# Splitting 544 tokens as 320 + 224 in place of 272 + 272 in a one-core decoder layer step

## The reference

```
h1 = LN1(ALPHA*x  + 0.5*SwiGLU_1(x))      # 1024 -> 2816 (twice) -> 1024
h2 = LN2(ALPHA*h1 + Mixer(h1))
y  = LN3(ALPHA*h2 + 0.5*SwiGLU_2(h2))
Mixer: z = h1 @ w_in -> pooled channels u, q (8 heads x 64), k, v (2 x 64), two gate vectors
  A: trailing means over 2/4/8/16 tokens minus the token, a 128x128 map per group, projection
  B: attention over the token and its 128 predecessors, rotary positions, sinks, projection
  out = (sigmoid(gA)*A + sigmoid(gB)*B) @ w_out
```

## Time and profile before

| | |
|---|---|
| runs timed | 1168.05 us and 4292.71 us |
| profiled execution: span | 1165.2 us |
| PE busy | 1136.7 us, 98% |
| PE weight loads busy | 1110.7 us, 95% |
| DVE busy | 556.8 us, 48% |
| ACT busy | 376.4 us, 32% |
| POOL busy | 149.6 us, 13% |
| mean granted TensorE clock | 0.991 |
| HBM traffic | 87 GB/s mean |

### The profile page before, as it was taken

How to read it: one execution, slowest core, us unless ns; L and a number is a source line. 1 busy time by engine, 2 the same in 40 slices (tenths; PEclk the granted TensorE clock), 3 DMA queues, 4 the chain that set the end, 5 groups by cost and what they waited for, 6 DMA issues and landing times.

```text
span 1165.2 us, 21801 instructions
## 1 busy us (share of the span) xinstructions
PE 1136.7 (98%) x8774; PEld 1110.7 (95%) x8774; DVE 556.8 (48%) x957; ACT 376.4 (32%) x676; POOL 149.6 (13%) x171
## 2 busy tenths in 40 slices
PE   6999999999999999999999999799999999999996
PEld 6999999999999989998899999699999999999994
DVE  3343433243443486877455555943443324444347
ACT  5222222122133334374442243422222222223334
POOL 2000000000002468400000015500000000000240
PEclk9999999999999989999999999999999999999998
DMA  9233441233333243221132332133243213234102
GB/s 250 73 91 90 124 134 56 73 91 91 95 107 88 70 120 74 76 64 37 46 91 73 96 105 78 50 91 89 78 119 94 73 56 109 79 90 132 43 1 77
DMA packets 191416, 101.16 MB, mean 87 GB/s; under 512 B 15129, under 2 KB 189453, under 8 KB 191320
## 3 DMA queue, kind: packets, MB, share of 16 engines
q1 hardware_dynamic: 189136, 95.77, 28.8%
q0 software_dynamic: 2208, 4.38, 1.2%
HBM read 97.63 MB, written 3.68 MB: 87 GB/s over the span
## 4 chain that ended last, share of the span: by engine, by line
PE 91%; DVE 6%; ACT 2%; issue 1%; DMA 0%; SPq 0%; DVEq 0%; ACTq 0%
PE psum L1157 29%; PE psum L1159 29%; PE psum L1158 28%; DVE y L868 1%; DVE act_lo L875 1%; PE psum L1341 1%; DVE y L849 1%; DVE ring_lo L788 1%; DVE stat L854 1%; PE psum L1357 1%; ACT ring_hi L528 0%; DMA xin<-in_x_prompt 0%; PE psum L1373 0%; DVE y L813 0%; PE psum L1269 0%
## 5 line engine op out<-in xcount | busy, mean ns | idle before, releaser
L1157 PE MATMUL psum<-act_hi,ring_hi 128*128 128x272 f32 x1824 | 532.0, 292 | 8.8 <-DVE act_lo L875 4.9
L1159 PE MATMUL psum<-act_hi,ring_lo 128*128 128x272 f32 x1824 | 530.3, 291 | 0.0
L1158 PE MATMUL psum<-act_lo,ring_hi 128*128 128x272 f32 x1824 | 527.0, 289 | 0.0
L1157 PEld LDWEIGHTS psum<-act_hi,ring_hi 128*128 128x128 f32 x1824 | 345.6, 189 | 17.7 <-DVE act_lo L875 9.3
L788 DVE TENSOR_TENSOR ring_lo<-raw,ring_hi 128x1024 fp32r<-128x1024 f32 (+1 forms) x170 | 202.0, 1189 | 305.7 <-ACT ring_hi L528 258.8
L1158 PEld LDWEIGHTS psum<-act_lo,ring_hi 128*128 128x128 f32 x1824 | 346.3, 190 | 0.0
L1159 PEld LDWEIGHTS psum<-act_hi,ring_lo 128*128 128x128 f32 x1824 | 345.4, 189 | 0.0
L528 ACT ACTIVATE ring_hi<-raw 128x1024 fp32r<-128x1024 f32 (+1 forms) x170 | 172.4, 1016 | 234.7 <-PE psum L1159 232.6
L568 ACT ACTIVATE tmp_a<-psum 128x272 f32<-128x272 f32 x184 | 73.2, 398 | 424.4 <-PE psum L1159 363.6
L1157 PE MATMUL psum<-hid_hi,ring_hi 128*128 128x272 f32 x512 | 148.6, 290 | 0.0
L1158 PE MATMUL psum<-hid_lo,ring_hi 128*128 128x272 f32 x512 | 147.0, 287 | 0.0
(11 more groups left out here) (185 smaller groups left out, 1184.6 us busy)
## 6 DMA issues: line engine op xcount, KB each, us to landing
raw<-in_ffn_w SPq DMA_DIRECT2D x176, 256.0 KB, 3.2
raw<-in_ffn_w SPq DMA_DIRECT2D x32, 512.0 KB, 4.0
raw<-in_w_in SPq DMA_DIRECT2D x52, 256.0 KB, 3.3
ext_raw<-in_ffn_w SPq DMA_DIRECT2D x32, 192.0 KB, 4.1
raw<-in_w_out SPq DMA_DIRECT2D x16, 256.0 KB, 3.2
raw<-in_w_pool_out SPq DMA_DIRECT2D x16, 128.0 KB, 2.3
raw<-in_w_attn_out SPq DMA_DIRECT2D x16, 128.0 KB, 2.7
xin<-in_x_prompt SPq DMA_DIRECT2D x3, 512.0 KB, 5.7
```

Source lines behind the costliest of these rows:

```text
L1157: pe.matmul(o, weights(s, k, True), x_hi[:, k, tok(c)], start=k == 0, stop=False)
L1158: pe.matmul(o, weights(s, k, True), x_lo[:, k, tok(c)], start=False, stop=False)
L1159: ins = pe.matmul(o, weights(s, k, False), x_hi[:, k, tok(c)], start=False, stop=k == kn - 1)
```

## The change

The cut between the chunks moves from token 272 to token 320. Chunk 0 has 320 tokens, chunk 1 has 224: 192 of the prompt and the 32 decoding ones. The token tiles of the transposes become 128, 128, 64 and 128, 64, 32 in place of 128, 128, 16 and 128, 112, 32. Scratch tiles get the width of the longer chunk and each use takes only its part. One ScalarE instruction that copied both chunks of a pooled group at once becomes two, one for each chunk. The number of matmuls, their order and their operand types stay.

```diff
-C = T // 2
+CUT = 320
+CHUNK = (CUT, T - CUT)
+CM = max(CHUNK)
...
-TOK_TILES = [(0, 128, 0), (128, 128, 0), (256, 16, 0), (272, 128, 1), (400, 112, 1), (512, 32, 1)]
+TOK_TILES = [(0, 128, 0), (128, 128, 0), (256, 64, 0), (320, 128, 1), (448, 64, 1), (512, 32, 1)]
...
-            return slice(c * C, c * C + C)
+            return slice(c * CUT, c * CUT + CHUNK[c])
...
-                    o = psum[:, bank, 0:C]
+                    o = psum[:, bank, 0:CHUNK[c]]
                     pe.matmul(o, weights(s, k, True), x_hi[:, k, tok(c)], start=k == 0, stop=False)
...
-                dve.tensor_tensor(tmp_v[:, c, :], psum[:, bank_of(at, c), 0:C], tmp_a[:, c, :], ALU.mult) \
+                dve.tensor_tensor(tmp_v[:, c, 0:CHUNK[c]], psum[:, bank_of(at, c), 0:CHUNK[c]], tmp_a[:, c, 0:CHUNK[c]], ALU.mult) \
...
-                        act.activation(scaled[:, slot, :].rearrange("p (c t) -> p c t", c=2), prod, ACT.Copy,
-                                       scale=pscale[:, g:g + 1]).then_inc(att_free, 1)
-                        act.activation(pz_hi[:, g, :].rearrange("p (c t) -> p c t", c=2), prod, ACT.Copy,
-                                       scale=pscale[:, g:g + 1]).then_inc(att_free, 1)
+                        for dst in (scaled[:, slot, :], pz_hi[:, g, :]):
+                            for c in range(2):
+                                ins = act.activation(dst[:, tok(c)], psum[:, 4 + 2 * i + c, 0:CHUNK[c]], ACT.Copy,
+                                                     scale=pscale[:, g:g + 1])
+                            ins.then_inc(att_free, 1)
...
-                        n = SEQ - C
+                        n = SEQ - CUT
...
-                        pe.matmul(psum[:, 4 + 2 * i, 0:C], w, z[:, BUF:BUF + C], start=True, stop=True)
-                        pe.matmul(psum[:, 5 + 2 * i, 0:n], w, z[:, BUF + C:BUF + SEQ], start=True, stop=True)
-                        ins = pe.matmul(psum[:, 5 + 2 * i, n:C], w, seg, start=True, stop=True)
+                        pe.matmul(psum[:, 4 + 2 * i, 0:CUT], w, z[:, BUF:BUF + CUT], start=True, stop=True)
+                        pe.matmul(psum[:, 5 + 2 * i, 0:n], w, z[:, BUF + CUT:BUF + SEQ], start=True, stop=True)
+                        ins = pe.matmul(psum[:, 5 + 2 * i, n:n + NS], w, seg, start=True, stop=True)
```

More of the change, by code:

```diff
@@ L142, in program @@
         soft = sb("soft", [P, 2, 6, H])
-        fsum = sb("fsum", [P, 2, C])
-        stat = sb("stat", [P, 2, C])
+        fsum = sb("fsum", [P, 2, CM])
+        stat = sb("stat", [P, 2, CM])
         table = sb("table", [P, 3])
[L146 to L149, removed]
+        p0 = sb("p0", [P, 4 * T])
+        tmp_a = sb("tmp_a", [P, 2, CM])
+        tmp_v = sb("tmp_v", [P, 2, CM])
+        sqs = [p0[:, 4 * CUT * c:4 * (CUT + CHUNK[1] * c)].rearrange("p (o t) -> p o t", o=4) for c in range(2)]
         tmp_r, scratch = stat[:, 1, :], stat[:, 0, 0:max(WINDOWS)]
@@ L430, in norm_sums @@
                         pool.wait_ge(shift_mm[c], l + 1)
-                    first = y[:, 0, tok(c)] if o == 1 else fsum[:, c, :]
-                    pool.tensor_tensor(fsum[:, c, :], first, y[:, o, tok(c)], ALU.add).then_inc(fsum_done[c], 1)
+                    total = fsum[:, c, 0:CHUNK[c]]
+                    first = y[:, 0, tok(c)] if o == 1 else total
+                    pool.tensor_tensor(total, first, y[:, o, tok(c)], ALU.add).then_inc(fsum_done[c], 1)
                 for k in range(1 if o == 3 else o, o + 1) if 3 <= o < KD - 1 else ():
@@ L436, in norm_sums @@
                         pool.wait_ge(sqsum_done[c], (KD - 2) * l + k - 1)
-                    total = sq[:, 4 * c, :]
-                    pool.tensor_tensor(total, total, sq[:, sq_slot(c, k), :], ALU.add).then_inc(sqsum_done[c], 1)
+                    total = sqs[c][:, 0, :]
+                    pool.tensor_tensor(total, total, sqs[c][:, sq_slot(c, k), :], ALU.add).then_inc(sqsum_done[c], 1)
             def all_norm_sums(l):
@@ L662, in epilogue @@
                     act.wait_ge(evac[c], u)
-                    act.activation(vT[:, tok(c)], psum[:, bank, 0:C], ACT.Copy).then_inc(evac[c], 1)
+                    act.activation(vT[:, tok(c)], psum[:, bank, 0:CHUNK[c]], ACT.Copy).then_inc(evac[c], 1)
                 elif U_GA <= m < U_PA:
@@ L666, in epilogue @@
                     act.wait_ge(evac[c], u)
-                    act.activation(m1[:, m - U_GA, tok(c)], psum[:, bank, 0:C], ACT.Sigmoid).then_inc(evac[c], 1)
+                    act.activation(m1[:, m - U_GA, tok(c)], psum[:, bank, 0:CHUNK[c]], ACT.Sigmoid).then_inc(evac[c], 1)
                 elif m >= U_GB and not is_proj(m):
@@ L813, in residual @@
                 dve.scalar_tensor_tensor(out=y[:, o, tok(c)], in0=y[:, o, tok(c)], scalar=factor,
-                                         in1=tmp_a[:, c, :], op0=ALU.mult, op1=ALU.add).then_inc(y_done[c], 1)
+                                         in1=tmp_a[:, c, 0:CHUNK[c]], op0=ALU.mult, op1=ALU.add).then_inc(y_done[c], 1)
             def deviation(l, c, o):
@@ L840, in norm_center @@
                 bank = stat_bank(l, c)
-                s = stat[:, c, :]
-                step(dve.tensor_tensor(s, psum[:, bank, 0:C], s, ALU.subtract))
+                s = stat[:, c, 0:CHUNK[c]]
+                step(dve.tensor_tensor(s, psum[:, bank, 0:CHUNK[c]], s, ALU.subtract))
                 step(dve.tensor_tensor(s, s, s, ALU.mult))
-                dve.tensor_tensor(s, psum[:, bank ^ 1, 0:C], s, ALU.subtract).then_inc(var_done[c], 1)
-                mean = psum[:, bank:bank + 1, 0:C].broadcast_to([P, 4, C])
+                dve.tensor_tensor(s, psum[:, bank ^ 1, 0:CHUNK[c]], s, ALU.subtract).then_inc(var_done[c], 1)
+                mean = psum[:, bank:bank + 1, 0:CHUNK[c]].broadcast_to([P, 4, CHUNK[c]])
                 for i in range(2):
@@ L953, in rotate @@
                     to = q + half if q % HD == 0 else q - half
-                    ins = dve.tensor_tensor(tmp_r[to:to + half], x[q:q + half, :],
+                    ins = dve.tensor_tensor(tmp_r[to:to + half, 0:CHUNK[c]], x[q:q + half, :],
                                             cos_sin[q:q + half, 1, tok(c)], ALU.mult)
                 step(ins)
-                dve.tensor_tensor(dst, tmp_v[:, c, :], tmp_r, ALU.add).then_inc(evac[c], 1)
+                dve.tensor_tensor(dst, tmp_v[:, c, 0:CHUNK[c]], tmp_r[:, 0:CHUNK[c]], ALU.add).then_inc(evac[c], 1)
             def epilogue(m, c):
@@ L971, in epilogue @@
                     dve.wait_ge(evac[c], u)
[L972 removed]
+                    prod = psum[:, bank_of(u, c), 0:CHUNK[c]]
+                    v = tmp_v[:, c, 0:CHUNK[c]]
                     if m < U_GB:
@@ L980, in epilogue @@
                         dve.wait_ge(m_done[c], o)
-                    dve.tensor_tensor(tmp_v[:, c, :], prod, tmp_a[:, c, :], ALU.mult).then_inc(evac[c], 1)
+                    dve.tensor_tensor(v, prod, tmp_a[:, c, 0:CHUNK[c]], ALU.mult).then_inc(evac[c], 1)
                     dve.wait_ge(evac[c], u + 1)
-                    step(dve.tensor_tensor(tmp_v[:, c, :], tmp_v[:, c, :], m1[:, o, tok(c)], ALU.add))
-                    step(dve.tensor_copy(m_hi[:, o, tok(c)], tmp_v[:, c, :]))
-                    dve.tensor_tensor(m_lo[:, o, tok(c)], tmp_v[:, c, :], m_hi[:, o, tok(c)], ALU.subtract) \
+                    step(dve.tensor_tensor(v, v, m1[:, o, tok(c)], ALU.add))
+                    step(dve.tensor_copy(m_hi[:, o, tok(c)], v))
+                    dve.tensor_tensor(m_lo[:, o, tok(c)], v, m_hi[:, o, tok(c)], ALU.subtract) \
                         .then_inc(m_done[c], 1)
@@ L1168, in shift @@
                 pe.wait_ge(consts_in, 16 * CONST_DMAS)
-                pe.matmul(psum[:, stat_bank(l, c), 0:C], mean_w[:, 0:P], fsum[:, c, :], start=True, stop=True) \
+                pe.matmul(psum[:, stat_bank(l, c), 0:CHUNK[c]], mean_w[:, 0:P], fsum[:, c, 0:CHUNK[c]], start=True, stop=True) \
                     .then_inc(shift_mm[c], 1)
@@ L1176, in stats @@
                 pe.wait_ge(fsum_done[c], (KD - 2) * (l + 1))
-                pe.matmul(psum[:, bank, 0:C], mean_w[:, 0:P], fsum[:, c, :], start=True, stop=False)
+                pe.matmul(psum[:, bank, 0:CHUNK[c]], mean_w[:, 0:P], fsum[:, c, 0:CHUNK[c]], start=True, stop=False)
                 pe.wait_ge(sqsum_done[c], (KD - 2) * (l + 1))
-                pe.matmul(psum[:, bank ^ 1, 0:C], mean_w[:, 0:P], sq[:, 4 * c, :], start=True, stop=False)
+                pe.matmul(psum[:, bank ^ 1, 0:CHUNK[c]], mean_w[:, 0:P], sqs[c][:, 0, :], start=True, stop=False)
                 pe.wait_ge(y_done[c], y_before(l) + KD)
-                pe.matmul(psum[:, bank, 0:C], mean_w[:, 0:P], y[:, KD - 1, tok(c)], start=False, stop=True)
+                pe.matmul(psum[:, bank, 0:CHUNK[c]], mean_w[:, 0:P], y[:, KD - 1, tok(c)], start=False, stop=True)
                 pe.wait_ge(sq_done[c], sq_op(l, KD - 1))
-                pe.matmul(psum[:, bank ^ 1, 0:C], mean_w[:, 0:P], sq[:, sq_slot(c, KD - 1), :], start=False,
```

(1 more changed line is left out.)

37 lines of the change are left out of this document (18 added, 19 removed).

## The result

The changed kernel takes 1195.59 us, median of two runs (1195.16 to 1196.02). Against the comparable runs of the kernel before it takes 1.0241 times as long, interval 1.022 to 1.0261: it is slower. The median of the two runs shown before, 2730.38 us, is no measure for this, since its run of 4292.71 us is left out of the ratio as not comparable. A second measurement, with seven runs of the kernel before on the same chip (median 1166.89 us), gives 1195.47 us and a ratio of 1.0247, interval 1.0229 to 1.0265. The profiled span grew from 1165.2 to 1194.2 us, by 29.0 us.

The account below looks back on a forecast made before the run. TensorE's matmul stream, with 91% of the chain of waits, was taken as the bound. Pairs 35.5 + norms 1.8 - tail 0.8 + start 0.4 = 37 us on 1168 gave 1205 us; range 1170 to 1232, likeliest 1188 to 1225.

Parts of the forecast that it names:

- wait saved at the second norm: TensorE reaches chunk 1's first tile 1.5 us later; 1.3 us of that taken as saved wait at each norm.
- The pair: Matmuls of 320 and 224 columns: 146.5 + 113 = 259.5 ns against 251.0, 8.5 more, times 4176: +35.5 us.
- The start: At the kernel's start the third token tile has 64 tokens, not 16, so its two copies take longer: +0.4 us.
- The norms: Mixer and second FFN starts: chunk 0's longer tiles and lost cover, less wait saved, 0.9 us each: +1.8 us.
- The tail: Chunk 1's bare norm at the end, 6.9 us, shortens 1.0 us; 0.2 returns through chunk 0's scaling: -0.8 us.
- Rival 1: fp32r load and matmul pair has a 125.5 ns floor: +44 us, 1213; upper bound +88 us, 1257; chance 0.22.
- Rival 2: 12 ns surplus comes from stream and load nearly tying at 272 columns: pair 246 ns, -21 us, 1148 to 1150; chance 0.17.
- Rival 3: Longer tiles draw out the lower clock after the norms: 5 to 15 us above forecast, up to 1220; chance 0.06.
- Rival 4: 224-column fp32r matmuls fall to fp32 speed, 373 ns each: +1.1 ms; chance 0.02.

Follow-up runs that it names:

- second profile: Profile of the changed kernel (320 + 224) measured once more, unchanged: 1195.47 us against 1166.89 us for the kernel before; profiled span 1193.4 us.

## Why the prediction was right or wrong

I predicted 1205 us, +37; it was 1195.6, about +28. The direction and the mechanism were right and the size was 9 us too high. The step that failed is the price of the pair, and in it the 113 ns for 224 columns; a second one is the wait saved at the second norm.

- **The pair.** I took 146.5 for 320 columns and 113 for 224, 8.5 ns more for the pair. Measured 146.6 and 111.5, 7.0 ns: 29 us in place of 35.5. The term that was off is the 3 ns that I added to the load's 110 for reading the moving operand beside it; 1.5 were there. The distances of loads are 111.5 ns beside 224 fp32r columns and 109.4 beside 96, which would fit such an addition, but no run shows that reading the operand is what causes it. The mechanism, load bound against column bound, is shown by the load that was halved on each side of the short matmul (109.0 and 55.8 ns).
- **The start.** I gave 0.4 us. The first matmul starts at 14.77 us in place of 13.68, +1.1, but at 13.99 in the second profile, +0.3; the rest is the wait for the input rows, 1.6 us in the one and 0.6 in the other. So the term was right. Up to the first sums another 0.7 to 0.9 us are more than the count of matmuls gives, and most of that lies in the first 24 matmuls: they take 8.3 us in place of 7.3 (8.5 in the second profile), where 24 x 21 ns are 0.5, because they run before the stream is at 125 ns a step, with steps of 227 ns before and 267 after.
- **The norms.** I gave +1.8 us for both. From the last sums of the mixer to the first sums of the second FFN, 355.8 us became 363.9, +8.1 (+8.7 in the second profile); its 1419 long and 1320 short matmuls alone account for 1419 x 21.1 - 1320 x 14.0 = +11.5. This border got about 3 us cheaper. The same count around the first norm gives +7.4 us against 7.3, and +6.0 in the second profile: nothing, or 1 us cheaper. The profile shows where the second border was cheapened. In the kernel before, TensorE waits there for chunk 1's tiles as well (window 745 to 762 us):

```profile
PE psum L1157 <- DVE act_lo L875: 1.7, 5, 0.4
```

  In the changed kernel the same place, 770 to 785 us, has no such wait in either profile. Counted by the steps, the time over 125.5 ns a matmul at this place was 4.7 us, 1.3 of them from steps at the lower clock; in the changed kernel it is 0.8 and 0.3 us over its own steps. I had put down 1.3 us of wait saved at each norm, and here it was about 4. (At the first norm 0.6 us of such waits went, and the 0.6 us for a weight tile came.) It is the right kind of term, too small: TensorE comes to these tiles later, and each is written sooner, since L871 and L878 are shorter at 224 columns. For chunk 0 they are longer, by 81 and 27 ns (588 and 548 before) where I took 50 for each, and counted in the same way the second border lost 0.3 us at chunk 0's tiles (1.6 in the second profile):

```profile
L871 DVE SCALAR_TENSOR_TENSOR y<-y,vecs,stat 128x320 f32<-128x320 f32 x16 | 10.4, 669 | 0.0
L878 DVE SCALAR_TENSOR_TENSOR act_lo<-y,vecs,act_hi 128x320 fp32r<-128x320 f32 x16 | 8.9, 575 | 0.0
L871 DVE SCALAR_TENSOR_TENSOR y<-y,vecs,stat 128x224 f32<-128x224 f32 x16 | 8.2, 532 | 0.2
L878 DVE SCALAR_TENSOR_TENSOR act_lo<-y,vecs,act_hi 128x224 fp32r<-128x224 f32 x16 | 7.1, 465 | 0.0
```

  How much of the 4 us each of the two causes gives was not tested by a run.
- **The tail.** From the last sums to the end it was 21.5 us and is 20.7: -0.8, as forecast. The second profile has 21.4, -0.1, so this term is not firmly shown.
- **Rival 1**, a floor of 125 ns: out, the short step is 111.5.
- **Rival 2**, a surplus from the near tie of load and columns: out. 320 columns, which outlast their load by far, keep 13 ns, and half a load beside 272 columns changes no step by more than 1.3.
- **Rival 3**, more of the lower clock: not shown. The stretch at 0.50 or 0.51 behind the first norm lasts 10.2 us in place of 6.8 in the profile shown, with steps of 266 ns for 320 columns, but 6.8 us in the second profile of the same kernel. Around the second norm it is 6.8 us in all three, in two pieces before and in one after. The length at the first norm varies from run to run by as much as the difference, about 1.5 us of time.
- **Rival 4**, short fp32r matmuls at fp32 speed: out.

Two rules of the Trainium skill stand beside these rows. The Trainium skill, "TensorE: Matmul & The Clock Gate", section "LDWEIGHTS", gives a weight load its columns / 1.2 ns, 53 and 107 for 64 and 128; the runs have 55.8 and 109, agreement within 3 ns. The Trainium skill, "TensorE: Matmul & The Clock Gate", section "Back-to-back issue gap", gives N / 2.4 + 2.5 for a matmul on its own, 216 ns for 512 columns; the fp32r stream has 232 here, so the formula does not carry over to it.

## What to carry to other kernels

In a stream where every matmul has a new weight, the price of a matmul is the larger of two: what its columns take, and the next matmul's weight load. Splitting a fixed number of columns unevenly costs little while both pieces stay above the load (2 us of 1168 for 288 + 256), and what a piece falls below it is lost: here the limit is near 240 columns for 128 fp32r weight columns. None of the three uneven splits tried was faster than 272 + 272. Read the pitch from starts, since the busy share of TensorE was 98% in both kernels.

## What the runs showed of the hardware

- In an fp32r stream a load of 128 weight columns of four bytes sets a step of 109 to 112 ns, one of 64 columns 56 ns. It is the load of the next matmul that counts; halving the matmul's own does nothing (109.0 against 109.4 ns).
- fp32r at the granted clock of 1.00: 111.9, 118.4, 125.5, 132.9, 140.1, 146.6 and 232.1 ns for 240, 256, 272, 288, 304, 320 and 512 columns, about 0.442 ns a column and 6 ns. At clock 0.51 it is 227 ns for 272 and 266 for 320, which is the columns at 1.2 GHz and nothing more.
- A bf16 matmul between fp32r ones made the kernel 2.8% slower: its load was not taken beside the fp32r matmul ahead of it.
- The start of a matmul's row does not say that it streams: after a matmul of 96 columns the next row begins 40 to 50 ns later, with a duration about 70 ns longer (0.36 against 0.29 us). Starts of weight loads, 109 ns apart, are the better measure there.
